# Blockwise inverse in a two-layer decoder trunk: products, copies and joins on half of the columns

## What is computed

```
a_mat = jnp.where(strict, jnp.einsum('bhnik,bhnjk->bhnij', k_beta, k) * decay, 0.0) + jnp.eye(C, dtype=f32)
tri = functools.partial(lax.linalg.triangular_solve, left_side=True, lower=True, unit_diagonal=True)
u = tri(a_mat, v * beta[..., None])
w = tri(a_mat, k_beta * jnp.exp(g)[..., None])
```

## Time and profile before

| | |
|---|---|
| Median of 3 runs | 1426.91 us (1426.12 to 1428.62) |
| Profiled execution, its own time | 1426.65 us |
| Its span, first to last instruction | 1424.9 us |
| Busy: PE, DVE, ACT, POOL | 1392.3, 670.4, 596.3, 523.3 us |
| Mean granted clock of TensorE | 0.998 of full speed |

### The profile page before, as it was taken

The page is one execution under the profiler, slowest core; times in us unless marked ns, Lnnn a source line. Parts: engine busy times, 40 slices in busy tenths (PEclk is TensorE's granted clock), DMA queues, the critical chain, the costliest instruction groups (busy, mean ns, idle before and its releaser), DMA issues.

```text
span 1424.9 us, 24940 instructions
## 1 busy us (share of the span) xinstructions
PE 1392.3 (98%) x10469; PEld 1144.5 (80%) x10469; DVE 670.4 (47%) x1112; ACT 596.3 (42%) x864; POOL 523.3 (37%) x239
## 2 busy tenths in 40 slices
PE   7999999999999999999999999999999999999998
PEld 5787778889878888888889967875688888888887
DVE  4666767788763314123143448856443223131231
ACT  5524763445644313222143555568635223141331
POOL 3544331111143443344335134232333533444341
PEclk9999999999999999999999999999999999999999
DMA  5332200000123322322324022210032223223221
GB/s 152 89 100 78 81 23 3 4 3 4 63 89 102 105 89 89 118 88 89 115 91 120 30 74 89 89 60 1 7 108 94 89 89 116 91 88 116 91 89 59
DMA packets 125857, 109.61 MB, mean 77 GB/s; under 512 B 6598, under 2 KB 123456, under 8 KB 125760
## 3 DMA queue, kind: packets, MB, share of 16 engines
q1 hardware_dynamic: 124880, 106.60, 23.7%
q10 hardware_dynamic: 880, 1.59, 0.3%
HBM read 106.08 MB, written 2.10 MB: 76 GB/s over the span
## 4 chain that ended last, share of the span: by engine, by line
PE 91%; DVE 3%; ACT 2%; issue 1%; POOL 1%; DMA 1%; SPq 0%; ACTq 0%; DVEq 0%; POOLq 0%
PE ps L569 22%; PE ps L571 22%; PE ps L570 22%; PE ps L713 5%; PE ps L1149 2%; PE ps L576 1%; PE ps L1159 1%; PE ps L577 1%; PE ps L581 1%; PE ps L1170 1%; PE ps L721 1%; PE ps L613 1%; POOL w_lo L2478 1%; PE ps L944 1%; PE ps L945 1%
## 5 line engine op out<-in xcount | busy, mean ns | idle before, releaser
L2478 POOL TENSOR_TENSOR w_lo<-lower,w_hi 128x2048 fp32r<-128x2048 f32 (+1 forms) x83 | 382.4, 4608 | 521.6 <-ACT w_hi L1241 506.8
L569 PE MATMUL ps<-h_hi,w_lo 128*128 128x512 f32 x648 | 253.7, 391 | 1.3 <-POOL w_lo L2478 1.2
L1241 ACT ACTIVATE w_hi<-lower 128x2048 fp32r<-128x2048 f32 (+1 forms) x83 | 157.6, 1899 | 226.2 <-PE ps L571 226.2
L570 PE MATMUL ps<-h_hi,w_hi 128*128 128x512 f32 x648 | 252.2, 389 | 0.0
L571 PE MATMUL ps<-h_lo,w_hi 128*128 128x512 f32 x648 | 252.2, 389 | 0.0
L569 PE MATMUL ps<-a_hi,w_lo 128*128 128x512 f32 x480 | 186.7, 389 | 0.0
L570 PE MATMUL ps<-a_hi,w_hi 128*128 128x512 f32 x480 | 186.7, 389 | 0.0
L571 PE MATMUL ps<-a_lo,w_hi 128*128 128x512 f32 x480 | 186.7, 389 | 0.0
L2185 DVE TENSOR_TENSOR lower<-lower,ps 128x512 f32<-128x512 f32 x60 | 41.2, 687 | 261.3 <-PE ps L571 240.3
L569 PEld LDWEIGHTS ps<-h_hi,w_lo 128*128 128x128 f32 x648 | 121.6, 188 | 30.0 <-POOL w_lo L2478 2.8
L2169 DVE SCALAR_TENSOR_TENSOR lower<-ps,lower 128x512 f32<-128x512 f32 x64 | 44.2, 691 | 213.4 <-PE ps L571 197.6
(11 more groups left out here) (415 smaller groups left out, 2197.7 us busy)
## 6 DMA issues: line engine op xcount, KB each, us to landing
lower<-in_mlp_w_dram SPq DMA_DIRECT2D x64, 1024.0 KB, 5.2
lower<-in_ev_w_in_dram SPq DMA_DIRECT2D x30, 512.0 KB, 3.8
lower<-in_od_w_in_dram SPq DMA_DIRECT2D x10, 1024.0 KB, 5.0
lower<-in_ev_w_out_dram SPq DMA_DIRECT2D x4, 1024.0 KB, 5.9
lower<-in_od_w_out_dram SPq DMA_DIRECT2D x4, 1024.0 KB, 5.0
out_dram<-lower SPq DMA_DIRECT2D x6, 256.0 KB, 2.5
upper<-in_x_dram SPq DMA_DIRECT2D x1, 1024.0 KB, 7.2
upper<-in_x_dram ACTq DMA_DIRECT2D x1, 1024.0 KB, 9.0
```

What stands on the lines that cost most here:

```text
L569: pe.matmul(o, wl, xh, start=(i_ == 0), stop=False)
L570: pe.matmul(o, wh, xh, start=False, stop=False)
L1241: act.activation(w_high(u)[:, :, 0:w], RAW[:, u % 2, :, 0:w], ACT.Copy).then_inc(hi_ready, 1)
L2478: pool.tensor_tensor(w_low(u)[:, :, 0:w], RAW[:, u % 2, :, 0:w], as_f32(w_high(u)[:, :, 0:w]), ALU.subtract)\
```

## The change

In the product `LT` x `TI` only the columns of every other block of `TI` are needed for the join. The change moves these alone. `every_other` picks, of 64 columns, those of every other block of size 2 << lev, so 32 columns; the 16 results of a group stand side by side in 256 columns of the bank. ACT copies 256 columns, the second product moves 32 columns a head, and DVE's predicated copy takes 256 columns from the bank into every other block of `TI`, which it walks in runs of b = 2, 4, 8 or 16 elements. In the last level the below product has 64 x 32 weights and 32 moved columns, the joined one 32 x 32 weights and 32 moved columns, and the copy goes to the second 32 columns of each head of `QI`. The transposes and all waits stay as they were.

```diff
+        def every_other(x, lev, first):
+
+            return x.rearrange("p (n u b) -> p n u b", u=2, b=2 << lev)[:, :, first, :]
+
+        def half_width(x):
+
+            return x.rearrange("p j q t -> p (j q t)")[:, 0:NH * HD // 2]
...
-                    both_halves(g, lt, ti, True).then_inc(inv_x, 1)
+                    for h_ in range(NH):
+                        j, q, at = h_ // 2, h_ % 2, h_ * HD // 2
+                        for part in HALVES:
+                            if lev < LAST - 1:
+                                mm = pe.matmul(ps[part, g, at:at + HD // 2], lt[part, j, q, :],
+                                               every_other(ti[part, j, q, :], lev, 0), start=True, stop=True)
+                            else:
+                                mm = pe.matmul(ps[part.start + HD // 2:part.stop, g, at:at + HD // 2],
+                                               lt[part, j, q, HD // 2:HD], ti[part, j, q, 0:HD // 2],
+                                               start=True, stop=True)
+                    mm.then_inc(inv_x, 1)
...
-                    if lev < LAST - 1:
-                        both_halves(g, qi[s % 2], xm, True).then_inc(inv_y, 1)
-                    else:
-                        both_halves(g, xm, qi[s % 2], True).then_inc(inv_y, 1)
+                    for h_ in range(NH):
+                        j, q, at = h_ // 2, h_ % 2, h_ * HD // 2
+                        for part in HALVES:
+                            if lev < LAST - 1:
+                                mm = pe.matmul(ps[part, g, at:at + HD // 2], qi[s % 2][part, j, q, :],
+                                               half_width(xm)[part, at:at + HD // 2], start=True, stop=True)
+                            else:
+                                low = slice(part.start + HD // 2, part.stop)
+                                mm = pe.matmul(ps[part.start:part.start + HD // 2, g, at:at + HD // 2],
+                                               half_width(xm)[low, at:at + HD // 2],
+                                               qi[s % 2][low, j, q, HD // 2:HD], start=True, stop=True)
+                    mm.then_inc(inv_y, 1)
...
-                    act.activation(flat4(xm), bank[g], ACT.Copy, scale=-1.0).then_inc(inv_xm, 1)
+                    act.activation(half_width(xm), bank[g][:, 0:NH * HD // 2], ACT.Copy, scale=-1.0).then_inc(inv_xm, 1)
...
-                    dve.copy_predicated(x, blocks(MERGE[:, lev + 1, :]), by_head(bank[g]))\
+                    u, b = int(not inner), 2 << lev
+                    new = x.rearrange("p j q (n u b) -> p (j q) n u b", u=2, b=b)[:, :, :, u, :]
+                    m = every_other(MERGE[:, lev + 1, :], lev, u).bitcast(I32).unsqueeze(1)
+                    dve.copy_predicated(new, m.broadcast_to([P, NH, HD // (2 * b), b]),
+                                        bank[g][:, 0:NH * HD // 2].rearrange("p (h n b) -> p h n b", h=NH, b=b))\
                        .then_inc(inv_t if inner else inv_done, 1)
```

## The result

The changed kernel took 1442.31 us (median of 6 runs, 1435.08 to 1444.27), the kernel before 1426.47 beside it (6 runs, 1425.78 to 1428.62): a ratio of 1.0102, 95% interval 1.0079 to 1.0126. It is 15.8 us slower. The forecast was 1419.5 with a range of 1414.5 to 1426, so its sign was wrong, and the range did not hold the time.

What follows compares the result with a forecast made beforehand. PE, busy 98% of the span, was taken as the bound. Waits in levels 0 to 3 (2.7 us) and level 4 (4.65) summed to 7.3 us off the profiled 1426.65, predicting 1419.5 us, range 1414.5 to 1426.

Steps and rivals of the forecast that it cites:

- The sum: Whole kernel: gains from waits in levels 0 to 3 and from level 4 together, 7.3 us.
- The clock: Rival: half clock stays down through levels 1 to 3 of a block, costing 11 us more; 1430.5 to 1453, 10%.
- the rival of single falls: Rival: one to three short clock falls around PE's waits, about 1.5 us lost each; 1421 to 1424, 15%.
- Copies and waits: Levels 0 to 3: ACT's copy falls to 0.38 us and DVE's to 0.45; shorter PE waits give 2.7 us.
- A product of levels 0 to 3: PE, levels 0 to 3: a product stays at 0.93 us with 32 moved columns, 58 ns a record.
- Level 4: Last level of each inverse: smaller weights make a product 0.50 us; 1.15, 0.94, 0.94 and 1.6 us saved, together 4.65.
- no product of levels 0 to 3 halved: Rival: moved columns set the record, so PE's products take 0.5 us in all levels; 1407, 7%.
- level 4 did shrink: Rival denied here: level 4 does not shrink because instructions may have a least time; 1422.5, or 1423.5 without PE gain, 15%.
- DVE gave nothing back: Rival denied here: DVE's steps from L1935 on give the gain back, within a microsecond or two of before; 5%.

Runs made afterwards that it cites:

- e1: Changed kernel, but levels 0 to 3 move 64 columns with full 512-column copies as before, so only level 4 is changed: 1422.83 us, ratio 0.9973.
- e6: Kernel before with only the ACT and DVE copies of levels 0 to 3 cut to 256 columns: 1423.57 us, ratio 0.9979.
- e9: Changed kernel, but joined products of levels 0 to 3 move 64 columns, below ones 32 (64 at level 0 of s = 0): 1420.05 us, ratio 0.9946.
- e10: Changed kernel, but in levels 0 to 3 the below products move 64 columns and the joined ones 32: 1420.71 us, ratio 0.9961.
- e3: Changed kernel, but both products of levels 0 to 3 move 64 columns; copies stay at 256, picked with a stride: 1418.85 us, ratio 0.9944.
- e4: Changed kernel with dense 512-column matmuls of constants where PE waits, in all four blocks: median 1419.91 us over ten runs, ratio 0.9985.
- e8: Changed kernel with two dense 512-column matmuls ahead of s = 0 alone: four runs 1426.40 to 1428.76 us, eight 1440.13 to 1441.95, ratio 1.0076.
- e13: Single profiled execution of the same program as e8 (changed kernel with the dense matmuls ahead of s = 0 alone): 1435.74 us.
- e5: Changed kernel, but below products of levels 0 to 3 move each head's first 32 columns side by side: 1441.69, 1441.88, 1442.08, 1430.17 us; ratio 1.0080.

## Why the prediction was wrong

**The step that failed is TensorE's clock.** The sum let every product run at the clock of before, and took the fall of the earlier trace rows as one that ends after 3.4 us whatever follows. The runs show that what follows decides: with products of 64 moved columns behind it (before, e1, e6, e9, e10) the fall ends after 3.4 us; with 32 in both products it lasted through the block, 34.1 us, and it made 11.5 of the 23.3 us that the changed kernel loses against e3. The clock stood among the rivals, with the right mechanism and nearly the right size (11 us a block staying down; s = 0 lost 11.5), but at the wrong place and chance. It was put behind the waits of s = 1 to 3 alone, where falls did come (6.8, 6.8 and 10.2 us), and not at s = 0, where the profile already showed one, and where half of the loss lay. That "the 32-column loads and matmuls still follow without a pause" was counted against it; they did follow so, and the clock stayed at half. The later blocks lost 5.4 (the last 4.6 us of the first stretch among it), 3.0 and 3.3, where the rival of single falls had about 1.5 for each, the price of a fall of 3.4 us (e10 measured 1.5), but these lasted 6.8 to 10.2. With 10% for the whole case the range stopped at 1426.

**Copies and waits: right.** ACT's copy was put at 0.38 us and took 0.382. DVE's took 0.43 for a forecast of 0.45, but 0.73 at level 0, in runs of two elements, which is the upper end that was named and not taken. The waits that they close were put at 2.7, and gave 2.9 (e6, medians).

**A product of levels 0 to 3: right.** 0.93 us was taken, and 0.94 measured at full clock. The weight load sets it, not the moved columns. The Trainium skill's page "TensorE: Matmul & The Clock Gate", section "LDWEIGHTS (loading the stationary operand)", has P / 1.2 ns for P weight columns, 53 ns for 64; the trace is near it with 58. By the N / 2.4 + 2.5 ns of its section "Back-to-back issue gap" the product would have halved; it did not. The prediction took that formula alone: the section calls it the gap of isolated matmuls, and says that in a stream of weight loads and matmuls both set the spacing, as this trace shows.

**Level 4: right.** 4.65 was predicted. By the marks of e1 it gave 4.6, by the medians 3.8 (e1 against before) and 4.7 (e3 against e6). By the marks the blocks gave 1.06, 1.05, 1.05 and 1.41 where 1.15, 0.94, 0.94 and 1.6 stood. A product was to be 0.50 us, and is 0.6 with its share of a restart. In s = 2 of the changed kernel, where the clock is up, DVE starts its next block (L1961, L1935 before) 3.7 us after the level's start; 4.1 was predicted.

**The sum: right where the clock holds.** 7.3 us were predicted. e3, with the same copies and level 4, gives 7.7 by the medians, and the changed kernel with the clock kept up ran at 1417.45 to 1420.13 in six of ten runs (e4).

**The other rivals** found nothing: no product of levels 0 to 3 halved, level 4 did shrink, and DVE gave nothing back.

What stays open: why the same program goes one way in one execution and the other in the next (e4, e8); whether a fall would end within levels that alternate 32 and 64 columns; and whether e9 or e10 would now and then fall as the changed kernel does in more runs than the 4 and 9 taken. e10's slowest two (1423.95 and 1424.52) have mean clocks of 0.995 and 0.994 against 0.997 in its profile, so they spent longer at half clock, where is not known.

## What to carry to other kernels

Before moved columns are cut from products whose time the weight load sets, ask what is gained: here nothing on PE, since a record stayed at 58 ns, while the clock lost what kept it up; cut the copies instead and leave the matmul wide (e3, 1418.85, beats both kernels). Where a profile shows a short fall of TensorE's clock, treat its return as part of the budget of whatever runs behind it. Read PE's records per microsecond and the granted clock, not its busy share.

## What the chip showed that was not expected

- The clock stayed at 0.50 for 34.1 us while PE was busy for 12.00 of 12 us by its records. It came back at 253.8, 4.6 us after the first product of 128 x 128 weights and 512 moved columns (L747, 249.23) had begun. In none of the 21 falls counted above did it come back within the 32-column products of levels 0 to 3.
- The same 32-column levels run at 1.00 from 281 to 293 us in the changed kernel, all through s = 0 in e4, and fall to 0.50 in their midst in e13 and e5. The two levels of the clock are both held there.
- Levels with 64 moved columns in one of the two products held 1.00 through s = 0 once it was up (e9, e10: 3.4 us down, as before, ended by products of 64 columns).
- DVE's predicated copy of 256 elements takes 0.73 us in runs of two elements, as long as 512 before, and 0.43 in longer runs; ACT's copy takes about the same either way (387 ns strided, 382 packed).
